# Hybrid convolution and sparse-attention layer on one core: x loaded first, modulation weights by channel, three projection tiles fed together, scores and counts placed later

## What is computed

```python
mod = jax.nn.silu(c) @ w_ada + b_ada                     # c: one vector, w_ada: 1024 x 3072
shift, scale, gate = jnp.split(mod, 3, axis=-1)
h = rmsnorm(x, norm_in) * (1.0 + scale[:, None, :]) + shift[:, None, :]
proj = h @ w_in                                          # 4680 columns
(cb, cc, cu, cz, aq, ak, av, az, iq, ik, iw) = jnp.split(proj, cuts, axis=-1)
y_conv = group_rmsnorm(short_conv_mixer(cb, cc, cu, conv_w, conv_b), gn_conv, 8) * silu(cz)
# indexer: q_idx from iq (8 heads), k_idx from ik, w_idx from iw; rotary on q, k, q_idx, k_idx
score = einsum('bqh,bqhs->bqs', wi_b, relu(einsum('bqhd,bsd->bqhs', qi_b, k_idx) * idx_scale))
_, sel = lax.top_k(where(causal, score, -inf), 256)      # attention only over the 256 best keys
y_attn = group_rmsnorm(softmax attention over sel, gn_attn, 8) * silu(az)
out = rmsnorm(x + gate * (concat(y_conv, y_attn) @ w_out), norm_f)
```

## Time and profile before

| | us |
|---|---|
| median of 3 runs | 781.19 |
| lowest, highest | 779.42, 783.22 |
| the profiled execution, its own time | 780.36 |
| its span, first to last instruction | 778.6 |
| PE busy in the span | 674.9 |
| DVE, ACT, POOL busy | 471.5, 360.5, 230.1 |

### The profile page before, as it was taken

The page is one execution under the profiler, slowest core; times in us unless marked ns, Lnnn a source line. Parts: engine busy times, 40 slices in busy tenths (PEclk is TensorE's granted clock), DMA queues, the critical chain, the costliest instruction groups (busy, mean ns, idle before and its releaser), DMA issues.

```text
span 778.6 us, 8765 instructions
## 1 busy us (share of the span) xinstructions
PE 674.9 (87%) x3170; PEld 550.7 (71%) x3170; DVE 471.5 (61%) x734; ACT 360.5 (46%) x542; POOL 230.1 (30%) x111
## 2 busy tenths in 40 slices
PE   0459993989999999639999999999889989879995
PEld 0447993768888888537887877787777777658884
DVE  3677822778889999955802210003788989566734
ACT  3554432755643223413244443344787877773211
POOL 0032322035324225531765656460011310030000
PEclk9967996999999999969999999999999999989998
DMA  8901189024325211100113411124964440211431
GB/s 341 367 28 54 48 218 154 1 81 136 103 88 165 80 55 54 33 22 28 54 63 128 162 55 32 50 64 104 297 154 113 111 106 4 57 55 68 174 109 54
DMA packets 22517, 79.14 MB, mean 102 GB/s; under 512 B 3722, under 2 KB 4042, under 8 KB 21452
## 3 DMA queue, kind: packets, MB, share of 16 engines
q1 hardware_dynamic: 22476, 78.60, 33.3%
HBM read 61.77 MB, written 13.41 MB: 97 GB/s over the span
## 4 chain that ended last, share of the span: by engine, by line
PE 55%; DVE 28%; DMA 5%; issue 5%; ACT 4%; SPq 2%; DVEq 0%; POOL 0%; ACTq 0%
PE ps L615 10%; PE ps L616 10%; PE ps L617 10%; DVE above L1232 7%; PE ps L790 4%; PE ps L792 4%; PE ps L791 4%; PE ps L728 3%; DMA xin<-in_x 2%; PE ps L673 2%; PE ps L674 2%; PE ps L654 2%; DMA iqs<-hlL 2%; PE ps L655 2%; DVE acc L1130 2%
## 5 line engine op out<-in xcount | busy, mean ns | idle before, releaser
L615 PE MATMUL ps<-hH,wH 128*128 128x512 f32 (+1 forms) x592 | 234.2, 396 | 8.4 <-DVE hL L430 4.4
L616 PE MATMUL ps<-hL,wH 128*128 128x512 f32 (+1 forms) x592 | 229.6, 388 | 0.0
L617 PE MATMUL ps<-hH,wL 128*128 128x512 f32 (+1 forms) x592 | 229.5, 388 | 0.0
L1451 POOL TENSOR_TENSOR wL<-raw,wH 128x1024 fp32r<-128x1024 f32 x37 | 93.7, 2534 | 219.1 <-ACT wH L852 219.0
L615 PEld LDWEIGHTS ps<-hH,wH 128*128 128x128 f32 x592 | 112.6, 190 | 33.9 <-issue 11.7
L617 PEld LDWEIGHTS ps<-hH,wL 128*128 128x128 f32 x592 | 112.7, 190 | 21.7
L616 PEld LDWEIGHTS ps<-hL,wH 128*128 128x128 f32 x592 | 113.1, 191 | 19.8 <-issue 1.0
L1317 DVE CUSTOM_DVE_ANT_0 ps<-ps,bias 128x128 f32<-128x128 f32 (+3 forms) x64 | 48.7, 761 | 57.1 <-PE ps L655 55.2
L1325 DVE TENSOR_TENSOR phL<-ps,phH 128x512 fp32r<-128x512 f32 (+1 forms) x96 | 52.7, 555 | 23.9 <-ACT phH L1007 19.1
L987 ACT ACTIVATE relu<-ps,wabs 128x384 f32<-128x384 f32 (+5 forms) x48 | 40.0, 849 | 46.8 <-PE ps L674 27.1
L1232 DVE TENSOR_SCALAR_CACHE_REDUCE above<-score,srch 128x384 bf16<-128x384 f32 (+5 forms) x60 | 56.8, 946 | 2.1
(11 more groups left out here) (193 smaller groups left out, 1073.5 us busy)
## 6 DMA issues: line engine op xcount, KB each, us to landing
raw<-in_w_units SPq DMA_DIRECT2D x36, 512.0 KB, 3.4
wa<-in_w_ada SPq DMA_DIRECT2D x8, 1024.0 KB, 13.3
ks<-qk_halves SPq DMA_DIRECT2D x32, 256.0 KB, 5.5
xin<-in_x SPq DMA_DIRECT2D x8, 512.0 KB, 12.5
gw<-in_w_ada SPq DMA_DIRECT2D x8, 512.0 KB, 4.9
qs<-qk_halves SPq DMA_DIRECT2D x16, 256.0 KB, 3.9
wo<-in_w_out SPq DMA_DIRECT2D x8, 512.0 KB, 9.2
xe<-in_x SPq DMA_DIRECT2D x8, 512.0 KB, 4.1
```

Of the source, the lines that this page charges most:

```text
L615: pe.matmul(out, wH[:, n % 2, kt, :], hH[:, kt, cols], start=(kt == 0), stop=False)
L616: pe.matmul(out, wH[:, n % 2, kt, :], hL[:, kt, cols], start=False, stop=False)
L617: mm = pe.matmul(out, wL[:, n % 2, kt, :], hH[:, kt, cols], start=False, stop=(kt == KT - 1))
L1451: g.tensor_tensor(wL[:, n % 2, :, :], raw[:, n % NRAW, :, :], wH[:, n % 2, :, :].bitcast(F32), ALU.subtract).then_inc(s_wL, 1)
```

## The change

- **Loads:** all of x first, then the first three weight tiles of the projection between the parts of `w_ada`. These are no longer rows by 2048 columns but four parts of 256 shift and 256 scale columns for all 1024 rows (2 MB each, in pieces of 1 KB). Parts 2 and 3 lie where x was, and are loaded once it is transposed.
- **Norm:** the root is taken for x in two groups of four tiles, and the transposes of the first three channel tiles start with the first group.
- **Modulation:** for each part DVE adds up seven row tiles, PE takes the eighth and the sum (`modulation(g)`), DVE finishes the factors of two channel tiles (`factors(g)`). h is formed by ACT, every `hL` by DVE.
- **Units 0 to 2** run together (`first_units(kt)`): each channel tile is multiplied into three PSUM pairs as it comes, with a third weight slot.
- **Positions** are loaded when two parts are done; their buffers have moved.
- **Scores:** blocks 2 to 7 in units 7 to 12, one each; both rotations of aq 0 and ak 0 ahead of the first block on DVE. `most` 0 behind cz 1 (unit 24), `most` 1 behind cc 2 (unit 25), `gate` behind cz 3, its loads two units later.
- **End:** the early output steps begin one chunk later, `head_out` of the last half goes ahead of the scalings on DVE, and the last output block goes through residual, square, norm and store in two halves, on DVE and ACT.

The diff, cut to its core:

```diff
-        ("aq", 0): [("idx", 2), ("idx", 3)],
-        ("ak", 0): [("idx", 4)],
-        ("aq", 1): [("idx", 5)],
...
+        ("ak", 0): [("idx", 2)],
+        ("aq", 1): [("idx", 3)],
...
-        ("cb", 0): [("most", 0)],
-        ("cz", 0): [("most", 1)],
-        ("cb", 3): [("gate", 0)],
+        ("cz", 1): [("most", 0)],
+        ("cc", 2): [("most", 1)],
+        ("cz", 3): [("gate", 0)],
...
-EARLY_PARTS = {3: 2, 4: 2, 5: 2, 6: 2, 7: 2, 8: 2, 10: 2, 11: 2}
+EARLY_PARTS = {4: 2, 5: 2, 6: 2, 7: 3, 8: 3, 10: 2, 11: 2}
...
+            for t in range(NB):
+                sp.dma_start(xin[:, t, :], a["x"][0, P * t:P * t + P, :]).then_inc(s_x[t], 16)
+            for g in range(NG):
+                if g < NFIRST:
+                    load(g)
+                if g == 2:
+                    sp.wait_ge(s_xtp, KT)
+                for part in range(2):
+                    sp.dma_start(wa[g][:, :, 2 * P * part:2 * P * part + 2 * P],
+                                 w_cols[:, :, D * part + 2 * P * g:D * part + 2 * P * g + 2 * P]).then_inc(s_wa[g], 16)
+            load(NFIRST)
+            sp.wait_ge(s_modp, 2)
             sp.dma_start(posi[:], a["positions"][0:1, :].broadcast_to([P, S])).then_inc(s_pos, 16)
...
+            def modulation(g):
+                pe.wait_ge(s_wa[g], 32)
+                for j in range(4):
+                    pe.matmul(ps[:, 6 + g % 2, j:j + 1], wa[g][:, KT - 1, P * j:P * j + P], csilu[:, KT - 1:KT], start=(j == 0),
+                              stop=False, skip_group_check=True)
+                pe.wait_ge(s_acc, (KT - 1) * (g + 1))
+                for j in range(4):
+                    mm = pe.matmul(ps[:, 6 + g % 2, j:j + 1], acc[g % 2][:, P * j:P * j + P], onesF[:], start=False, stop=True,
+                                   skip_group_check=True)
+                mm.then_inc(s_modp, 1)
...
+                for n in range(NFIRST):
...
+                    for half in range(2):
+                        out = ps[:, 2 * slot(n) + half, 0:w]
+                        pe.matmul(out, wH[slot(n)][:, kt, :], hH[:, kt, cols], start=(kt == 0), stop=False)
+                        pe.matmul(out, wL[slot(n)][:, kt, :], hH[:, kt, cols], start=False, stop=False)
+                        mm = pe.matmul(out, wH[slot(n)][:, kt, :], hL[:, kt, cols], start=False, stop=(kt == KT - 1))
...
+            modulation(0)
+            for kt in range(KT):
+                first_units(kt)
+                if kt % 2 == 0 and kt // 2 + 1 < NG:
+                    modulation(kt // 2 + 1)
...
+            split_high(2)
             for kt in range(KT):
+                act.wait_ge(s_amp, kt // 2 + 1)
+                A(xT[:, kt, :], xT[:, kt, :], ACT.Identity, bias=shift[:, kt:kt + 1], scale=amp[:, kt:kt + 1]).then_inc(s_h, 1)
                 act.wait_ge(s_h, kt + 1)
                 A(hH[:, kt, :], xT[:, kt, :], ACT.Copy).then_inc(s_hH, 1)
...
+            for g in range(NG):
+                for k in range(KT - 1):
+                    if g and k == 3:
+                        factors(g - 1)
+                    ada_sum(g, k)
+                if g:
+                    low_h(2 * g - 2)
+                    low_h(2 * g - 1)
+            factors(NG - 1)
+            low_h(KT - 2)
+            low_h(KT - 1)
```

More of the change, by code:

```diff
@@ L424, in wait_low, with raw_count @@
                 waits.wait_ge(s_splP, m + 1 - NT)
[L426 to L430, removed]
+        def raw_count(n):
+            return 1 if n < NFIRST else (n - NFIRST) // 2 + 2
         block = ctx.enter_context(nc.Block())
@@ L563, in _ @@
             sp.dma_start(gate[:], dgate.rearrange("(o n) -> o n", o=1).broadcast_to([P, D])).then_inc(s_gate, 16)
-            for b in range(NB):
+            for b in range(NB - 1):
                 sp.wait_ge(s_fin, b + 1)
@@ L569, in _ @@
                     sp.dma_start(xe[:, b % 2, :], a["x"][0, P * (b + 2):P * (b + 3), :]).then_inc(s_xe[b % 2], 16)
-            for i in range(2):
-                sp.wait_ge(s_out[i], 16 * (NB // 2))
+            for half in range(2):
+                sp.wait_ge(s_finh[half], 1)
+                cols = slice(HALF * half, HALF * half + HALF)
+                sp.dma_start(a["out"][0, P * (NB - 1):P * NB, cols], oe[:, 1, cols]).then_inc(s_out[1], 16)
+            sp.wait_ge(s_out[0], 16 * (NB // 2))
+            sp.wait_ge(s_out[1], 16 * (NB // 2 + 1))
         @block.tensor
@@ L590, in _, with turn_x @@
-            for j in range(2 * KT):
-                mm = pe.matmul(ps[:, 0, j:j + 1], acc[:, P * j:P * j + P], onesF[:], start=(j == 0), stop=True,
-                               skip_group_check=True)
-            mm.then_inc(s_modp, 1)
+            def turn_x(kt, t):
+                return pe.transpose(two(2 * (kt % 3))[:, P * t:P * t + P], xin[:, t, P * kt:P * kt + P], identF[:])
+            for lo_t, hi_t in X_GROUPS:
+                pe.wait_ge(s_xn, hi_t)
+                for kt in range(3):
+                    for t in range(lo_t, hi_t):
+                        mm = turn_x(kt, t)
+                    if hi_t == NB:
+                        mm.then_inc(s_xtp, 1)
@@ new lines, in _ @@
+            for kt in range(3, KT):
+                pe.wait_ge(s_xt, kt - 2)
+                for t in range(NB):
+                    mm = turn_x(kt, t)
+                mm.then_inc(s_xtp, 1)
+            def modulation(g):
[8 more added lines that the diff above has]
+                mm.then_inc(s_modp, 1)
@@ L835, in _, with split_high, square @@
             A(csilu, vec[:, V_C:V_C + KT], ACT.Silu).then_inc(s_csilu, 1)
-            for t in range(NB):
+            def split_high(n):
+                act.wait_ge(s_raw[slot(n)], 16 * raw_count(n))
+                if n >= NFIRST:
+                    act.wait_ge(s_unit, earlier(n) + 1)
+                A(wH[slot(n)][:], raw[slot(n)][:], ACT.Copy).then_inc(s_wH, 1)
+            def square(t):
                 act.wait_ge(s_x[t], 16)
@@ L1094, in _, with last_block @@
             pair_root(NT - 1, 1)
+            def last_block():
+                for half in range(2):
+                    act.wait_ge(s_resh, half + 1)
+                    cols = slice(HALF * half, HALF * half + HALF)
+                    A(xe[:, 1, cols], te[:, 1, cols], ACT.Square, accum_out=finh[:, half:half + 1]).then_inc(s_fsq, 1)
+                act.wait_ge(s_fv, NB)
+                A(finr[:, NB - 1:NB], fin[:, NB - 1:NB], ACT.Sqrt, scale=1.0 / D, bias=vec[:, V_EPS:V_EPS + 1]).then_inc(s_fs, 1)
+                act.wait_ge(s_fr, 1)
+                act.wait_ge(s_rnh, 2)
+                A(oe[:, 1, HALF:D], oe[:, 1, HALF:D], ACT.Copy, scale=finr[:, NB - 1:NB]).then_inc(s_finh[1], 1)
             for b in range(NB):
@@ L1410, in _ @@
                     low_y(2, 0)
+                    low_y(3, 0)
+            head_out(2 * NH - 1)
             for t in range(NT - 1):
```

269 lines of the change are left out of this document (147 added, 122 removed).

## The result

| | before | after |
|---|---|---|
| median, us | 780.64 (4 runs) | 751.84 (751.17 to 752.88, 4 runs) |
| the profiled execution: time, span | 780.36, 778.6 | 751.63, 749.8 |
| granted clock, mean | 0.957 | 0.972 |
| PE, DVE, ACT, POOL busy | 674.9, 471.5, 360.5, 230.1 | 678.5, 470.7, 371.5, 221.9 |

The account below looks back on a forecast made before the run. The time was taken as the start of the units plus PE's work plus the holes in it. Gains of 10.1 + 19.3 + 5.5 = 34.9 us against 780.4 us gave 745.5 us, range 733 to 759.

Parts of the forecast that it names:

- The sum: Whole kernel: gains of 10.1 + 19.3 + 5.5 = 34.9 us against 780.4 us, giving 745.5 us.
- Start: Up to units 0 to 2: x normed at 23.3 us, first unit matmul about 40, those units done at 79, not 90.
- my 4 us: DVE stalls beside POOL's three early splits: 4 us allowed, against 7 to 8 us if each cost its whole length.
- (e): Rival at the start: strided `w_ada` parts load at 118 GB/s, the time is 773 us; slower from 102 GB/s; chance 0.03.
- The ring: Units 0 to 2: modulation, factors, sums, `hL` and matmuls cycle over two channel tiles, 10.3 us each.
- Where the lead goes: From angles to first score: chain 4.5 us later, unit 5 at 112.3, `iqs` at 138.8, wait before scores closed; gain 10.1 us.
- the signs: Traces that would show it right, among them none or 1 to 2 us of PE wait before the first score.
- chain 12 us later: Rival at the start: `w_ada` parts at half rate or factors waiting for small matmuls; 755 to 760 us; chance 0.17.
- Search and counts: Units 13 to 24: search, slowed about 10 us, ends near 363, PE needs it at 373; wait gone, gain 19.3 us.
- The end: Behind attention: early output steps 1.0 us, square wait and clock 2.5 of 7, last block 2.0; gain 5.5 us, from 1 to 9.
- The last block: Last output block in halves: 3.6 instead of 5.6 us from last matmul to store, gain 2.0 us.

Follow-up runs that it names:

- sched_only: Kernel before with only the places of scores, rotations and counts (`most`, `gate`) changed; start, loads and end as before; 749.21 us, ratio 0.9584.
- tail_fix: Changed kernel with POOL's two late weight splits given to DVE, and the last half's `pair_gate` and `pair_add` ahead of DVE's output weight splits; 743.35 us, ratio 0.9510.
- tail_only: Kernel before with only the changes behind attention: later early output steps, last `head_out` ahead of scalings, last output block in halves; 778.45 us, ratio 0.9968.
- tail_fix_again: tail_fix unchanged, measured again in the third group on another chip; 743.51 us, ratio 0.9523 to the kernel before.
- old_start: tail_fix with the start of the kernel before in place of the new one; 740.29 us, ratio 0.9481 to the kernel before.
- raw_angles_split: tail_fix with unit 5's load ahead of the `kiH`/`kiL` copies, six angle operations earlier, unit 5's high split ahead of ACT's evacuation of unit 3; 735.62 us, ratio 0.9423.

## Right and wrong, by the steps of the prediction

**Right in the sign and the size, 6.3 us short.** The errors do not cancel: two terms fell short, and the largest came out right. The sum charged the new start with 4.5 us (10.9 - 4.5), took the gain from the scores and counts, and that is how it is: sched_only alone is as fast as the change. I had not said plainly that this makes the start a loss; the runs do.

**Start.** Norming 22.3 for 23.3: the second four took 4.83 us, the first four 2.74, 2.1 us of stall beside POOL where I had 2. The last of the three early splits stretched one small operation (L1227, 0.91 us for 0.16), the second found DVE idle: 2.9 us in all. (The sum charges 2 us for this, in the norming, though the text beside the rule speaks of "my 4 us".) The 7 to 8 us that the prediction worked out from the rule in the Trainium skill, page "SBUF — State Buffer", section "Who interferes with whom", were for the case that every split meets DVE's work, and that was not so. The parts of `w_ada` landed as said (DVE took up part 1 at 29.75 us, 29.8 forecast), so (e) falls: 349 GB/s. The ring took 9.65 us, not 10.3. The angles came 3.1 us later, not 5.6. These small errors all lean one way: units 0 to 2 end at 77.5 us (79 forecast) and unit 5 starts 1.6 us ahead of the forecast. I left out that three units which finish together leave no free weight slot, so that PE stood 5.0 us between 77.5 and 83.1 us. That cost nothing here, since PE had 8.0 us left to wait at unit 5.

**Where the lead goes.** I put one delay, 4.5 us, on unit 5 and on `iqs` alike. They moved by 2.9 and 6.1. The step that failed is that the wait before unit 5 has a price of its own: after 8.0 us of standing the clock was 0.89 for the unit, 12.3 us instead of 10.9, 1.4 us that I had granted to other waits and not to this. And PE waited 2.8 us at the first score where the sum had nothing and the signs none to 2. The relu wait fell from 3.8 to 0.7, which looks like more than the half that I gave it, but it is the wait for `iqs` that took its place: the mechanism, both rotations ahead of the scores, shows no saving, for the wait stays at 3.7 to 3.8 in four profiles with the new order, and in tail_fix it is the rotation of ak 0 that stands before it. 8.2 us for 10.1. The rival "chain 12 us later" was not met.

**Search and counts.** The term is right within 0.6 us, and its reasoning half wrong. I added ten POOL operations to the search. There were 27 in both (before 51.7 us of POOL from 227.7 to 342.5, after 50.8 from 241.3 to 349.9): the convolution's came in, two `hlL` splits of POOL went out. The search got 6.2 us shorter, not 10 longer. As the cover was 10 us, the error cost nothing.

**The end.** This is the term that was mis-sized most: 5.5 us forecast, 1.1 in the two profiles, 2.9 by the medians of tail_only. I saw that `pair_add` would be late beside POOL's splits, put its end "near 697 at best" on the clock of before, 3 us of wait, and took 2.5 us as gain. On that clock it ended at 698.5 (670.8 + 27.7), PE waited 4.9, and the half clock for 6.1 us came back with it. The wait of 1.8 us for `yH` in the early steps did go; 0.9 of it went into the longer wait, and the other 0.8 I cannot place. Of the 2.5 us, 1 was the shorter wait and 1.5 a part of the clock, for which I had no row. The last block gained 0.9, not 2.0, in this profile: the store's issue came 3.4 us behind the last matmul, as said (3.6), but 3.1 us from issue to end became 4.4. That is the one exception. In the ten other profiles with this end the last block takes 6.7 to 6.9 us, not 7.9 (8.8 before), so the 2.0 us of the forecast were right; in after the last store landed 3.2 us behind its issue, in the others 2.3.

**The chances.** The rivals leave 0.04 for "same" and "slower" together (0.03 in (e) and 0.01), where the forecast has 0.05.

## What to carry to other kernels

A lead that is won at the start has to be followed through the next units until something uses it: here PE spent 5.0 us of it when three weight slots fell free together and 8.0 us at one load queued behind eight copies on SP. Only the second was the bound; moving that load brought unit 5 4.3 us nearer to unit 3. A wait of zero does not say how much slack is behind it, and a wait that is shortened but not removed can keep its clock penalty. Before an operation is moved ahead on an engine, read what stands between it and the buffer that its consumer needs; up to the last matmul, moving `pair_add` and POOL's two splits was worth 6.9 us, moving the head alone 0.1 and 1.6 in two profiles.

## What the runs showed that I had not expected

- Loads of `w_ada` in pieces of 1 KB over 128 partitions, with weight tiles among them, ran at 349 GB/s with the DMA share at 1.10; x in pieces of 4 KB ran at 419 with 1.02 (from 9 to 12 us). A quarter of the piece went with a sixth less rate.
- The time of the `iqs` copies differs between executions. The changed kernel and tail_fix are the same up to there; one came to the first score at 137.5 us and waited until 140.4, the other came at 138.3 and did not wait. One trace is not enough to call such a wait a bound.
- The first unit with the old start began at 51.6, 53.2, 52.5, 51.8 and 54.1 us in five profiles, and unit 3 with the new start at 83.1, 82.5, 83.9, 82.5, 82.7 and 82.1 in six: single profiles of one start differ by up to 2.5 us.
- The same wait does not always cost the clock the same. Behind a wait of about 3.1 us for relu the granted clock stayed at 1.00 in tail_fix and was 0.50 for 3 us in sched_only, tail_fix_again and old_start; 2.1 us before unit 5 in raw_angles_split were followed by 0.50 too. From unit 7 to unit 13 PE took 101.6 us in the four profiles with scores in units 7 to 12 whose clock stayed up, 102.9 to 103.1 in the five where it fell for some 3 us, and 104.2 in old_start, where it fell for some 7. So differences of 1 to 3 us between single profiles of these kernels can be the clock alone.
